# Weight sums of a half-product scheme built in DRAM by accumulating transfers, the same scheme for the up tiles, and a norm moved behind the down product

## The reference

```python
hn = rms_norm(h, ffn_norm_g[l])            # per token: h * rsqrt(mean(h*h) + eps) * g
h  = h + (silu(hn @ w_ffn_gate[l]) * (hn @ w_ffn_up[l])) @ w_ffn_down[l]
```

## Time and profile before

| | |
|---|---|
| time, median of 3 | 1477.91 us (1476.44 to 1479.18) |
| span of the profiled execution | 1474.7 us |
| instructions | 21908 |
| busy share PE, PEld, DVE, ACT, POOL | 99%, 83%, 65%, 41%, 12% |
| DRAM traffic by transfers | 132.99 MB, 90 GB/s on average |

### The profile page before, as it was taken

The page is one execution under the profiler, slowest core; times in us unless marked ns, Lnnn a source line. Parts: engine busy times, 40 slices in busy tenths (PEclk is TensorE's granted clock), DMA queues, the critical chain, the costliest instruction groups (busy, mean ns, idle before and its releaser), DMA issues.

```text
span 1474.7 us, 21908 instructions
## 1 busy us (share of the span) xinstructions
PE 1463.0 (99%) x8052; PEld 1231.0 (83%) x8052; DVE 960.8 (65%) x1747; ACT 608.4 (41%) x1067; POOL 179.3 (12%) x164
## 2 busy tenths in 40 slices
PE   9999999999999999999999999999999999999998
PEld 8867786888888898898898777777888888988987
DVE  6678986575884587387844472524758855873875
ACT  4234446535442343244511464444344423432444
POOL 2023325100000000000004663220000000000000
PEclk9999999999999999999999999999999999999999
DMA  7534310133333332332333202221433333333322
GB/s 180 151 85 143 112 51 1 37 107 100 100 101 94 106 101 86 100 115 81 92 90 82 57 10 78 59 64 36 114 90 98 98 101 114 95 92 100 115 72 101
DMA packets 250613, 132.99 MB, mean 90 GB/s; under 512 B 21273, under 2 KB 247701, under 8 KB 250526
## 3 DMA queue, kind: packets, MB, share of 16 engines
q1 hardware_dynamic: 248302, 123.92, 29.4%
q0 software_dynamic: 2144, 7.77, 1.9%
q10 hardware_dynamic: 80, 0.14, 0.0%
HBM read 129.67 MB, written 6.38 MB: 92 GB/s over the span
## 4 chain that ended last, share of the span: by engine, by line
PE 95%; DVE 2%; DMA 1%; ACT 1%; issue 1%; SPq 0%; DVEq 0%; POOL 0%; ACTq 0%
PE psL L2163 52%; PE psS L2186 12%; PE psL L2388 12%; PE psS L2163 5%; PE psT L2397 2%; PE psL L2523 1%; PE psS L2704 1%; PE psS L2438 1%; PE psL L2659 1%; PE psS L2496 1%; PE psS L2682 1%; PE psS L2630 1%; PE psS L2425 1%; DMA stage<-in_w_out 1%; DMA xin<-in_x 0%
## 5 line engine op out<-in xcount | busy, mean ns | idle before, releaser
L815 ACT ACTIVATE wh<-stage 128x1024 fp32r<-128x1024 f32 (+3 forms) x229 | 222.4, 971 | 373.0 <-PE psL L2163 268.0
L2163 PE MATMUL psL<-hn,wh 128*128 128x512 f32 x1104 | 342.8, 392 | 0.0
L1282 DVE TENSOR_TENSOR wl<-stage,wh 128x1024 fp32r<-128x1024 f32 (+2 forms) x186 | 206.0, 1108 | 74.2 <-ACT wh L815 73.9
L2163 PEld LDWEIGHTS psL<-hn,wh 128*128 128x128 f32 x1104 | 204.7, 188 | 44.4 <-issue 3.3
L2163 PE MATMUL psL<-hn,wl 128*128 128x512 f32 x552 | 215.0, 389 | 0.0
L2163 PE MATMUL psL<-hid,wh 128*128 128x512 f32 x680 | 209.4, 389 | 0.0
L2388 PE MATMUL psL<-hn,wh 128*128 128x512 f32 x496 | 165.0, 414 | 0.2 <-DVE yn L2048 0.2
L2163 PEld LDWEIGHTS psL<-hid,wh 128*128 128x128 f32 x680 | 127.5, 188 | 26.7
L2163 PE MATMUL psL<-hid,wl 128*128 128x512 f32 x340 | 132.3, 389 | 0.0
L2163 PEld LDWEIGHTS psL<-hn,wl 128*128 128x128 f32 x552 | 103.6, 188 | 22.0
L678 POOL TENSOR_TENSOR wl<-stage,wh 128x1024 fp32r<-128x1024 f32 (+1 forms) x43 | 97.7, 2272 | 197.7 <-ACT wh L815 197.7
(11 more groups left out here) (465 smaller groups left out, 2591.9 us busy)
## 6 DMA issues: line engine op xcount, KB each, us to landing
stage<-in_w_in SPq DMA_DIRECT2D x53, 512.0 KB, 3.7
stage<-in_w_ffn_gate SPq DMA_DIRECT2D x22, 512.0 KB, 3.6
stage<-in_w_ffn_up SPq DMA_DIRECT2D x22, 512.0 KB, 3.8
stage<-in_w_ff_gate SPq DMA_DIRECT2D x22, 512.0 KB, 3.7
stage<-in_w_ff_up SPq DMA_DIRECT2D x22, 512.0 KB, 3.6
stage<-in_w_out SPq DMA_DIRECT2D x16, 512.0 KB, 4.0
stage<-in_w_ffn_down SPq DMA_DIRECT2D x16, 512.0 KB, 4.0
stage<-in_w_ff_down SPq DMA_DIRECT2D x16, 512.0 KB, 3.9
```

The costliest lines, as they stand in the source:

```text
L815: act.activation(wh[:, b, 0:n], stage[:, b, 0:n], ACT.Copy).then_inc(hi[b], 1)
L1282: v.tensor_tensor(wl[:, b, 0:n], stage[:, b, 0:n], wh[:, b, 0:n].bitcast(F32), ALU.subtract).then_inc(lo[b], 1)
L2163: ins = pe.matmul(dst, w[:, b, k * P:(k + 1) * P], x[:, part, k, c0:c1], start=k + n == 0, stop=k == kc - 1 and n == 2)
```

## The change

- **Weight sums.** For each block, matrix (gate, up) and sum (two) a DRAM tensor of 1024 x 1408 is filled by POOL's transfers: for each part of the feed-forward width 16 transfers (`SUM_DMAS`), eight plain copies DRAM to DRAM and then eight with `accum_op=ADD`. Each has 512 rows of 256, 512 or 384 columns (parts a, b, c: 512, 1024 and 768 KB). For part a of either block the first eight go without waits between them, then four together, then two and two. For parts b and c each one waits for all before it. Block 1's part a stands between the low parts of `gates1`, and its last two ahead of `mask_bias`. Part b's first eight stand in `mask_bias`, one after every fourth unit, and the rest and part c come after it. Block 2's stand between and behind the low parts of `gates2`. DVE's `weight_sums` is gone. SP loads the sums into `wsum`.
- **Pairs.** A pair is now tile t and tile t + 11 (the two halves of the width), and both matrices go by seven half products: `tile_pair`, a gate pair in the banks of psS, then the up pair in psL and psT. `hid_slot` orders the hidden tiles so, and the down weights come with two transfers a slot (`load_down`). A pair's loads are 512 KB, 512 KB of sums, 256 KB, 512 KB of sums. The four plain tiles of part a stay.
- **Norm.** The up tile is no longer multiplied by R. `add_down` multiplies the down tile by R into `ft` and then adds it to `hT`; `add_last` the same. The sign of three token sums is turned.
- Some semaphores are merged or dropped; POOL's `gates2` loop is unrolled.

```diff
+SUM_DMAS = 16
+SUMS_AT = (0, 2, 3, 4, 5, 6, 8, 12, 14)
...
+            def load_pair(name, i, q, l, m, pair):
+                w = by_rows(w_ffn[l, m])
+                load(name, i, 0, w, pair * P)
+                if q:
+                    sp.wait_ge(ws_lo, 2 * q - 1)
+                sp.dma_start(wsum[:, 0:2 * SEQ].rearrange("p (k n) -> p k n", n=P), by_rows(w_sums[l, m, 0])[:, :, pair * P:(pair + 1) * P]).then_inc(ws_in[0], 16)
+                sp.wait_ge(lo[1], PAIR0[name] + i)
+                sp.dma_start(stage[:, 1, SEQ:2 * SEQ].rearrange("p (k n) -> p k n", n=P),
+                             w[:, KD // 2:, (FPAIRS + pair) * P:(FPAIRS + pair + 1) * P]).then_inc(w_in[1], 16)
+                if q:
+                    sp.wait_ge(ws_lo, 2 * q)
+                sp.dma_start(wsum[:, 2 * SEQ:].rearrange("p (k n) -> p k n", n=P), by_rows(w_sums[l, m, 1])[:, :, pair * P:(pair + 1) * P]).then_inc(ws_in[1], 16)
...
+                    sp.wait_ge(sums_in, 16 * SUM_DMAS * (3 * l - 3 + part + 1))
...
+            def sum_dmas(l, part, first, last):
+                before = SUM_DMAS * (3 * l - 3 + part)
+                t0, t1 = summed_pairs(part)
+                cols = slice(t0 * P, t1 * P)
+                second = slice((FPAIRS + t0) * P, (FPAIRS + t1) * P)
+                upper, lower = slice(0, D // 2), slice(D // 2, D)
+                for n in range(first, last):
+                    if before + n and (n in (0, 8, 12, 14) or (l, part) not in ((1, 0), (2, 0))):
+                        pool.wait_ge(sums_in, 16 * (before + n))
+                    m = "gu"[n % 2]
+                    w, s12, s43 = w_ffn[l, m], w_sums[l, m, 0], w_sums[l, m, 1]
+                    to, src = ((s12[upper, cols], w[upper, second]), (s43[lower, cols], w[upper, cols]),
+                               (s12[lower, cols], w[lower, second]), (s43[upper, cols], w[lower, cols]),
+                               (s12[upper, cols], w[lower, second]), (s43[lower, cols], w[upper, second]),
+                               (s12[lower, cols], s43[lower, cols]), (s43[upper, cols], s12[lower, cols]))[n // 2]
+                    if n < 8:
+                        pool.dma_start(to, src).then_inc(sums_in, 16)
+                    else:
+                        pool.dma_start(to, src, accum_op=ALU.add).then_inc(sums_in, 16)
...
+                sum_dmas(1, 0, SUMS_AT[i], SUMS_AT[i + 1])
...
+            sum_dmas(1, 0, 14, SUM_DMAS)
             for j in range(len(la_units)):
                 mask_bias(j)
+                if j % 4 == 3:
+                    sum_dmas(1, 1, j // 4, j // 4 + 1)
+
+            sum_dmas(1, 1, 8, SUM_DMAS)
+            sum_dmas(1, 2, 0, SUM_DMAS)
...
+                sum_dmas(2, 0, SUMS_AT[i], SUMS_AT[i + 1])
+            sum_dmas(2, 0, 14, SUM_DMAS)
+            sum_dmas(2, 1, 0, SUM_DMAS)
+            sum_dmas(2, 2, 0, SUM_DMAS)
...
-                v.tensor_tensor(hT[:, n, :], hT[:, n, :], psL[:, b, :], ALU.add).then_inc(ev[b], 1)
+                v.tensor_tensor(ft[:, 2 * b, :], psL[:, b, :], R, ALU.mult).then_inc(upper_ok, 1)
+                v.wait_ge(upper_ok, 2 * i + (2 * gate_pairs_before(l, part + 1) + down_before(l, part) + b + 1))
+                v.tensor_tensor(hT[:, n, :], hT[:, n, :], ft[:, 2 * b, :], ALU.add).then_inc(ev[b], 1)
...
-            def gate_pair(name, i, n, l):
+            def tile_pair(l, part, e, i, q, up):
...
                 half_product(x, first, 0, rows_of(0, 0)).then_inc(acc_x, 1)
-                half_product(psS[:, 1, 0:HT], first, SEQ, rows_of(KD // 2, 0)).then_inc(mm[0], 1)
+                pe.wait_ge(ws_lo, 2 * q + 1)
+                pe.wait_ge(xt_lo, 4 * l)
+                half_product(y, mixed, 0, token_sums(0)).then_inc(acc_y, 1)
+                half_product(x1, first, SEQ, rows_of(KD // 2, 0)).then_inc(mm[0], 1)
...
                 half_product(x, mixed, 3 * SEQ, token_sums(2), add=True).then_inc(acc_x, 1)
-                for b in range(2):
-                    product(name, i + 1, b, hn)
```

More of the change, by code:

```diff
@@ L473, in heads_bank, with pair_banks @@
             return psT[:, i, :] if m == 3 and i < 2 else psS[:, i - 2, :] if m == 3 else psS[:, i, :]
+        def pair_banks(up):
+            return (psL[:, 1, 0:HT], psL[:, 0, 0:HT], psT[:, 0, 0:HT], psT[:, 1, 0:HT]) if up else [psS[:, n, 0:HT] for n in range(4)]
         def last_bank(half, b):
@@ L1133, in swiglu @@
                     elif part == 2:
                         high(f"dn{l}c", 0, 1)
[L1135 removed]
+                    if up:
+                        inner_high(i - 1, part, f0)
+                    else:
+                        act.wait_ge(gate_ok, q + 1)
+                        act.activation(ft[:, 1, :], ft[:, 0, :], ACT.Tanh, scale=0.5).then_inc(t_ok, 1)
+                second_tile(*entries[-1])
             branches(1)
@@ new lines, in last_steps @@
+                def last_steps(i, q, up):
+                    if up:
+                        inner_low(i - 1, part, f0)
+                        inner_low(i, part, f0, inner2[:])
+                    else:
+                        for m in range(2):
+                            v.wait_ge(t_ok, f0 + i + m + 1)
+                            v.scalar_tensor_tensor(out=ft[:, 2 * m, :], in0=(ft[:, 1, :], tanh2[:])[m], scalar=1.0, in1=ft[:, 2 * m, :],
+                                                   op0=ALU.add, op1=ALU.mult)
@@ new lines, in swiglu @@
+                for e, (i, q, up) in enumerate(entries):
+                    last = e == len(entries) - 1
+                    _, x1, y, _ = pair_banks(up)
+                    sum_ = ft[:, 3 if up else 0, :]
+                    if e:
+                        second_tile(*entries[e - 1])
+                    sum_low(q, 1)
+                    if e:
+                        last_steps(*entries[e - 1])
+                    done(name, i, 0)
+                    v.wait_ge(out_x, 2 * q + 1)
+                    v.tensor_tensor(sum_[:, 0:HT], x1, part_x[:, 0:HT], ALU.add).then_inc(ev[0], 1)
+                    low_next(name, i, last)
+                    if not last:
+                        sum_low(q + 1, 0)
+                        second_low(name, i + 1)
@@ L2142, in _, with product @@
         def _(pe):
-            def product(name, i, b, x, meta=0, made=None, between={}):
+            def product(name, i, b, x, meta=0, made=None, between={}, order=None):
                 pe.wait_ge(lo[b], PAIR0[name] + i + 1)
@@ L2156, in product @@
                         pe.wait_ge(mlo, meta - 1)
-                    for k in range(kc):
+                    for done_, k in enumerate(order or range(kc)):
                         if (m, k) in between:
@@ L2735, in _ @@
             first = PAIRS[name] - 1
-            product(name, 0, 0, hid, made=(hid_lo, before_part(2, 2)))
+            product(name, 0, 0, hid, made=(hid_lo, before_part(2, 2)), order=[hid_slot(2, i) for i in range(FPARTS[2])])
             product(name, 0, 1, hid)
```

317 lines of the change are left out of this document (164 added, 153 removed).

## The result

The changed kernel takes 1515.99 us (median of 4 runs, 1508.75 to 1519.0) against 1477.18: ratio 1.026 (95% interval 1.023 to 1.029). The forecast was 1473.5 with a range of 1464 to 1491. The profiled execution spans 1517.0 us against 1474.7, 42.3 us more.

What follows compares the result with a forecast made beforehand. PE was taken as the bound, busy 99% of the span. Terms -15.1 + 3.1 + 0.6 + 5.0 + 2.0 = -4.4 us gave 1473.5 against 1477.91; own range 1469 to 1478, full range with rivals 1464 to 1491.

Steps and rivals of the forecast that it cites:

- Loads beside the sums: Two output-weight loads on the chain lose 1 us each beside transfers, 2.0 us (0 to 4); others have slack.
- three signs that the prediction names for being wrong: An accumulation over 2.4 times a copy's data time, a copy over 6.7 us, or a copy under 5.
- the forecast's fixed 2.2 us: The part of a 1024 KB copy's 6.0 us that is not data time, given as 2.2 to 2.4.
- The pairs: Feed-forward: 18 pairs of up tiles go from 10.91 to 10.07 us, 15.1 us less, with no new wait.
- The copies and accumulations: Sum transfers of 1024 KB: a copy takes 6.0 us, an accumulation 10.0; block 2's sums arrive in time.
- R = 237: Latent attention: time in us of part b's first copy, once all of block 1's part a has landed.
- slow copies: Rival: copies pace the latent attention at 7.9 us each, +7.0 us in all, 1485; chance 0.15.
- slow accumulations: Rival: accumulations take three times the data time, delaying latent attention and block 2's part c, +32, 1510; chance 0.17.
- The latent attention: Mask biases wait behind POOL's copies; unit 28 is 7.7 us late, of which 5.0 us stay on the path.
- the forecast's sign: Latent attention: DVE's unit 28 comes at about 275 with POOL's bias as releaser, not PE.
- The norm: Block 1's part c down product: an extra DVE multiplication per tile makes the next norm's squares 3.1 us later.
- the 0.6 us: Block 2's part c down product: only the last half tile's multiplication and its twin count, 0.6 us.

Runs made afterwards that it cites:

- experiment 1: Changed kernel, POOL holding the rest of block 1's part b sums and all of part c until the branch products are done: 1484.42 us, ratio 1.007.
- experiment 2: Kernel before, with scratch transfers of 1024 KB added beside block 1's branch products: eight accumulations 1500.24 us, four 1483.59, eleven plain copies 1480.31.
- experiment 5: Transfers of half the size: kernel before with sixteen added accumulations of 512 KB, 1482.08 us; changed kernel with each sum transfer halved, 1486.76 us.
- experiment 6: On top of experiment 1, the eight part b copies between the latent attention's mask biases are held back too: 1480.97 us, ratio 1.003.
- second version of experiment 8: Changed kernel, sums moved to stretches without short loads, three copies put behind block 1's branches, parts c's norm multiplied into the gate: 1468.48 us, ratio 0.994.

## Why the prediction was wrong

**The step that failed** is "Loads beside the sums ... 1 us each, 2.0 us ... Other loads have 3 us or more of slack". It looked at the loads that were on the chain already; for the 3 us of the others it shows no row, and the only slack that it works out is that of the feed-forward network. The branch products have 12 matmuls a tile, so a load comes every 2.8 us and has 1.1 us of slack. And the price of company was taken as 1 us, where such a load landed only when the transfer beside it had: 2.8 us became 7.5 to 8.8. Measured 35.0 us in place of 2.0. Experiments 1, 2 and 5 show it from three sides: take the transfers away, add them to the kernel before, keep their bytes and halve their size. None of the three signs that the prediction names for being wrong came. In the median a copy took 5.3 us (between 5 and 6.7), and with the forecast's fixed 2.2 us an accumulation's data time is by estimate 6.9 against 3.1, 2.2 times (under 2.4). For br1 it had no rival.

**The pairs** were right: 14.3 us of 15.1 came. PE's only new wait there is 0.5 us for `part_x`, and the loads had the room that was claimed, except where accumulations of 1024 KB came every 9 to 12 us beside them (experiment 6, and the second version of experiment 8).

**The copies and accumulations** were right in size: part b's first copy was issued at 236.6 (R = 237 forecast), in the changed kernel copies of 1024 KB landed in 5.2 to 7.6 us, median 5.3, and accumulations in 8.4 to 11.5, median 9.1 (6.0 and 10.0 forecast), and the sums were in time for gu2b and gu2c, where PE doesn't wait. The Trainium skill's half rate for a reduction ("Collectives: The Full Stack", section "The bandwidth ceiling") fits roughly: 9 us against 5.3 here, 1.7 times. The Trainium skill's fit that gives 4.4 us by estimate for a copy ("DMA: Bandwidth & Descriptors", section "Anatomy of one DMA") was below every copy of this size that I read. The two rivals on slow copies and slow accumulations did not happen.

**The latent attention** came later than forecast, 8.8 us against 5.0, and not where it was forecast. POOL's order was right: one copy for four units of biases, 5.5 to 6.9 us apart where 6.0 was reckoned, the seventh at 271.8 (273 forecast). POOL of the changed kernel:

```profile
236.61 0.67 POOL L770 DMA_DIRECT2D weight_sums_1g<-in_w_ffn_gate  x1 [6.38 <-DMA weight_sums_1u<-weight_sums_1u]
...
242.13 0.64 POOL L770 DMA_DIRECT2D weight_sums_1u<-in_w_ffn_up  x1 [3.12 <-DMA weight_sums_1g<-in_w_ffn_gate]
...
247.80 0.62 POOL L770 DMA_DIRECT2D weight_sums_1g<-in_w_ffn_gate  x1 [2.35 <-DMA weight_sums_1u<-in_w_ffn_up]
```

But the forecast looked at unit 28 alone. By its own schedule the biases of units 12 and 20 are ready at about 250 and 263, some 7 and 9 us behind DVE's times in the kernel before, so the wait comes early. DVE of the changed kernel, units 8, 12 and 28:

```profile
243.62 0.44 DVE L1692 CUSTOM_DVE_ANT_0 W<-psS,biasM 128x272 f32<-128x272 f32 x1 [2.34 <-POOL biasM L815]
...
249.28 0.44 DVE L1692 CUSTOM_DVE_ANT_0 W<-psS,biasM 128x272 f32<-128x272 f32 x1 [2.64 <-POOL biasM L815]
...
278.34 0.71 DVE L1692 CUSTOM_DVE_ANT_0 W<-psS,biasM 128x528 f32<-128x528 f32 x1 [1.36 <-PE psS L2623]
```

Unit 28 waits for PE, as long as it did before, and not for POOL, as the forecast's sign had it: it is late because units 8 and 12 were. What the 8.8 us are made of can be read off. PE waits 6.0 us in this stretch, 0.4 in the kernel before:

```profile
PE psT L2524 <- ACT W L1048: 4.3, 5, 2.2
PE psS L2623 <- DVE negm L1692: 1.3, 1, 1.3
PE psT L2524 <- DVE m L1766: 0.4, 1, 0.4
```

And behind one of these waits (1.4 us, until 244.8) the granted clock is 0.66 from 245 to 255 us, where PE is busy 9.6 of 10 us and which by estimate costs another 3.4: 5.6 + 3.4 = 9.0. So the waits come near the 5.0 forecast, by another road, which is luck, and the clock was not reckoned.

**The norm** was right for dn1c as far as DVE goes, and the stretch took 7.8 us more against 3.1. DVE of the changed kernel, one tile:

```profile
746.07 0.68 DVE L2023 TENSOR_TENSOR ft<-psL,Rk 128x512 f32<-128x512 f32 x1
746.79 0.69 DVE L2025 TENSOR_TENSOR hT<-hT,ft 128x512 f32<-128x512 f32 x1
747.40 0.95 DVE L1393 TENSOR_TENSOR wl<-stage,wh 128x768 fp32r<-128x768 f32 x1
748.27 0.75 DVE L1840 SCALAR_TENSOR_TENSOR hn<-hT,g,hn 128x512 fp32r<-128x512 f32 x1
749.41 1.23 DVE L1835 TENSOR_TENSOR sqacc<-sqacc,tmp 128x1024 f32<-128x1024 f32 x1 [0.38 <-ACT tmp L1264]
```

From start to start 4.48 us (4.43 forecast), of which 0.38 is not DVE's work but a wait for ACT's squares. DVE's lag holds back the low parts too: kv2's first product comes 1.3 us late, and behind it PE waits 2.1 us for DVE's `hn`. That is 3.4, near the 3.1 forecast, and it is the same 3.4 in experiment 1. The rest goes with the clock: behind PE's waits the granted clock was 0.63 in this stretch of the changed kernel, and 0.86 in the one behind it:

```profile
765.00:775.00 10.00, 8.01 (x38) 7.99 (x39) 5.82 (x19) 2.80 (x4) 0.00 (x0) 0.63 0.23 70
```

By estimate that is 3.7 + 1.4 = 5.1 us, and 8.5 with the waits, against 7.8 measured. In experiment 1 the granted clock was 0.83 over 10 us (730 to 740), 1.7 us, and dn1c with the step took 5.2 us more, near 3.4 + 1.7. In dn2c the 0.6 us was 2.8, with the granted clock at 1.00: there the chain of the last pairs goes from PE over the multiplication, the addition, ACT and DVE's low part back to PE, each pair.

**A sum.** The forecast's own range, "1469 to 1478", is by its terms 1470.3 to 1478.5 (copies 5.8 to 6.5 us, load waits 0 to 4). Nothing hangs on it.

## What to carry to other kernels

Before a spare queue is given work, list every stretch that it will lie beside, and for each the slack of its shortest load: time between two loads of a slot, less landing, less the steps to the consumer. Count a load beside a foreign transfer in rows of 2 KB as landing when that transfer has landed. Then the size of one background transfer, more than the bytes in all, sets the price: keep its time under the consumer's own period, or keep it out of that stretch. A multiplication moved behind a product is free only where its engine has slack in that very stretch, up to the last tile. And when an engine's deliveries are late, compare every one of them with the time it is wanted, not the last alone.

## What was unexpected of the hardware

In br1 a load of 256 KB took 2.8 us alone. Of the two that alternate, the one on the chain took 4.2 us in the median beside copies of 1024 KB in 2 KB rows, 7.5 to 8.8 beside accumulations of 1024 KB (the other 6.4 to 7.2), 4.4 beside accumulations of 512 KB (the other 3.1), and 6.6 to 7.3 beside copies in rows of 512 bytes. Over all runs an accumulation of 1024 KB in DRAM in rows of 2 KB took 8.3 to 12.1 us, a copy 5.1 to 9.2; in rows of 512 bytes, beside br1, 11.4 to 14.0 and 7.2 to 8.1. PE's waits cost twice where the granted clock fell behind them: 3.4 us in the latent attention and 5.1 at kv2, by the estimates above. Left open: why a load is held back at first and goes packet for packet later. With accumulations in 512-byte rows the loads got 1023 packets beside 1707 from 312 to 319 us, so holding back is not complete there, and the count of one pair for each transfer does not give that run's 24 us.
